# Feed-forward by seven products: products that add onto a bank, and a new order of the products

## What is computed

```python
def modulate(x, shift, scale):
    return x * (1 + scale) + shift

def swiglu(x, w13, w2):
    a, b = jnp.split(x @ w13, 2, axis=-1)
    return (jax.nn.silu(a) * b) @ w2

def ffn_half_step(h, g, shift, scale, gate, w13, w2):
    return h + 0.5 * gate * swiglu(modulate(rms_norm_2(h, g), shift, scale), w13, w2)
```

## Time and profile before

| what | us |
|---|---|
| median of 3 runs | 4607.99 |
| range of the runs | 4604.65 to 4612.93 |
| the profiled execution, its own time | 4617.37 |
| its span from first to last instruction | 4615.6 |
| TensorE busy in it | 4242.2 (92%) |
| weight loads busy | 3445.0 (75%) |
| VectorE busy | 2458.5 (53%) |
| ScalarE busy | 1471.4 (32%) |

### The profile page before, as it was taken

The page is one execution under the profiler, slowest core; times in us unless marked ns, Lnnn a source line. Parts: engine busy times, 40 slices in busy tenths (PEclk is TensorE's granted clock), DMA queues, the critical chain, the costliest instruction groups (busy, mean ns, idle before and its releaser), DMA issues. The chain is left out here.

```text
span 4615.6 us, 89015 instructions
## 1 busy us (share of the span) xinstructions
PE 4242.2 (92%) x39320; PEld 3445.0 (75%) x39320; DVE 2458.5 (53%) x3948; ACT 1471.4 (32%) x2591; POOL 94.3 (2%) x83
## 2 busy tenths in 40 slices
PE   7999999998869999799998998999989999988997
PEld 4666666667547777499997556999989999446886
DVE  4455554545122333276764353766676665345886
ACT  3323322332023444143332232333343332223443
POOL 0000000000000000000000020000000000020000
PEclk9999999999889999899999999999999999998998
DMA  3000000002343443212121101122112121202221
GB/s 143 22 22 22 22 22 21 3 22 80 132 160 147 165 157 137 109 65 73 65 74 44 67 19 55 65 74 74 55 55 77 61 73 39 100 19 80 94 101 64
DMA packets 42479, 332.02 MB, mean 72 GB/s; under 512 B 4082, under 2 KB 8563, under 8 KB 12787
## 3 DMA queue, kind: packets, MB, share of 16 engines
q1 hardware_dynamic: 42098, 326.37, 19.5%
HBM read 324.26 MB, written 2.10 MB: 71 GB/s over the span
## 5 line engine op out<-in xcount | busy, mean ns | idle before, releaser
L762 PE MATMUL banks<-x_hi,w_hi 128*128 128x384 f32 (+1 forms) x2496 | 812.5, 326 | 50.8 <-ACT ffn_tiles L879 33.6
L763 PE MATMUL banks<-x_lo,w_hi 128*128 128x384 f32 (+1 forms) x2496 | 806.9, 323 | 0.0
L764 PE MATMUL banks<-x_hi,w_lo 128*128 128x384 f32 (+1 forms) x2496 | 806.7, 323 | 0.0
L849 ACT CAST w_hi<-landing 128x512 fp32r<-128x512 f32 x768 | 466.5, 618 | 625.2 <-PE banks L764 615.9
L928 DVE TENSOR_TENSOR w_lo<-landing,w_hi 128x512 fp32r<-128x512 f32 x768 | 519.4, 685 | 72.5 <-ACT w_hi L849 69.3
L762 PEld LDWEIGHTS banks<-x_hi,w_hi 128*128 128x128 f32 x2496 | 475.5, 191 | 65.1 <-ACT ffn_tiles L879 46.3
L763 PEld LDWEIGHTS banks<-x_lo,w_hi 128*128 128x128 f32 x2496 | 475.5, 191 | 0.2
L764 PEld LDWEIGHTS banks<-x_hi,w_lo 128*128 128x128 f32 x2496 | 475.3, 190 | 0.0
L762 PE MATMUL banks<-g_hi,w_hi 128*128 128x384 f32 (+1 forms) x1232 | 421.2, 342 | 0.0
L763 PE MATMUL banks<-g_lo,w_hi 128*128 128x384 f32 (+1 forms) x1232 | 421.2, 342 | 0.0
L764 PE MATMUL banks<-g_hi,w_lo 128*128 128x384 f32 (+1 forms) x1232 | 421.2, 342 | 0.0
(11 more groups left out here) (419 smaller groups left out, 6067.2 us busy)
## 6 DMA issues: line engine op xcount, KB each, us to landing
landing<-in_w SPq DMA_DIRECT2D x132, 1024.0 KB, 4.9
arena_first<-in_ada_w SPq DMA_DIRECT2D x44, 2048.0 KB, 7.9
weight_ring_first<-in_rw_pair SPq DMA_DIRECT2D x8, 2048.0 KB, 8.8
weight_ring_first<-in_da_head SPq DMA_DIRECT2D x8, 2048.0 KB, 12.4
weight_ring_mix<-in_w_in SPq DMA_DIRECT2D x12, 1024.0 KB, 5.0
weight_ring_first<-in_ada_w SPq DMA_DIRECT2D x4, 2048.0 KB, 8.7
weight_ring_mix<-in_w_out SPq DMA_DIRECT2D x8, 1024.0 KB, 4.9
x_res<-in_x_t SPq DMA_DIRECT2D x2, 2048.0 KB, 12.2
```

The costliest lines, as they stand in the source:

```text
L762: mm(o, wh, xh, start=first, stop=False, skip_group_check=onto)
L763: mm(o, wh, xl, start=False, stop=False, skip_group_check=onto)
L764: return mm(o, wl, xh, start=False, stop=last, skip_group_check=onto)
L849: nc.scalar.copy(SH[:, q % RING], raw(q)).then_inc(whi.h, 1)
```

## The change

It changes which bank a product is made in, which engine sums, and the order of the products. Nothing is left out and no product is added.

- Three banks a group. P1 is made in bank 0 and ScalarE copies it to X1; P6 adds onto it and ScalarE copies the sum to X2; P7 adds onto it and ScalarE copies that to X3; P4, whose weights now have the opposite sign (t4 is b21 - t2), adds onto it and ScalarE takes the silu from the bank. P2 has bank 1. P5 has bank 2 and P3 adds onto it.
- VectorE adds three times in place of six: bank 1 onto X1 after P2, bank 2 onto X3 after P7 and onto X2 after P3. The two gatings follow P3.
- The order is P1, then P4 and P3 of the group before, then P2, P6, P5, P7. With a "w" unit in between, P4 and P3 follow its first slot. Slots keep their old places in the ring; `order` lists them as they are used.
- The ring is refilled by `splits_at`: after place n come those slots, in slot order, whose predecessor in the ring has been used by then. VectorE does the same one place later.

```diff
@@ -660,8 +661,9 @@
         PLAIN, RING, GR = 2, 11, 6
         A11, A21, A12, A22, S1, S2, S4 = range(7)
         S3 = A21
+        P1, P3, P2, P5, P6, P7, P4 = range(7)
         operand_of = (A11, S4, A12, S1, S2, S3, A22)
-        bank_of = (0, 1, 0, 2, 3, 4, 5)
+        bank_of = (0, 2, 1, 2, 0, 0, 0)
 
...
-        used_up = lambda q: last_slot[slots[q][3]] + 1 if slots[q][0] == "g" and slots[q][1] < PLAIN else q + 1
+        order, held = [], []
+        for kind, u in units:
+            q = begin[kind, u]
+            if kind == "g" and u < PLAIN:
+                order += [q, q + 1, q + 2, q + 3]
+            elif kind == "g":
+                order += [q + P1] + held + [q + P2, q + P6, q + P5, q + P7]
+                held = [q + P4, q + P3]
+            else:
+                order += [q] + held + list(range(q + 1, q + (8 if u < 5 else 4)))
+                held = []
+        assert sorted(order) == list(range(Q))
+        place_of = {q: n for n, q in enumerate(order)}
+        used_up = lambda q: place_of[last_slot[slots[q][3]] if slots[q][0] == "g" and slots[q][1] < PLAIN else q] + 1
+        ended = lambda kind, u, part: place_of[begin[kind, u] + part] + 1
+        splits_at, nxt = [], RING
+        for n in range(Q):
+            splits_at.append([])
+            while nxt < Q and used_up(nxt - RING) <= n + 1:
+                splits_at[-1].append(nxt)
+                nxt += 1
+            assert n + 1 == Q or order[n + 1] < nxt
...
         first_bank, at_bank = {}, 0
         for kind, u in units:
+            if kind == "w":
+                at_bank += at_bank % 2
             first_bank[kind, u] = at_bank
-            at_bank += 16 if kind == "w" else 4 if u < PLAIN else 6
+            at_bank += 16 if kind == "w" else 4 if u < PLAIN else 3
         bank_no = lambda kind, u, n: (first_bank[kind, u] + n) % 8
...
-                def group(u):
-
-                    q, s = begin["g", u], u - PLAIN
-                    for part in range(7):
-                        b, x = bank_no("g", u, bank_of[part]), operand_of[part]
-                        if part != 2:
-                            take_bank(b, *((sil_ready, 2 * u + 1), (u_made, 6 * s + 3), None, (u_made, 6 * s + 5), (u_made, 6 * s + 1),
-                                           (u_made, 6 * s + 4), (u_made, 6 * s + 6))[part])
-                        else:
-                            pe.wait_ge(p1_copied.h, p1_copied.at(0, s + 1))
-                        if s == 0 and part == 1:
-                            pe.wait_ge(sums_lo.h, sums_lo.at(0, 4))
-                        if s == 0 and part == 5:
-                            pe.wait_ge(sums_lo.h, sums_lo.at(0, 5))
-                        pe.wait_ge(wlo.h, wlo.at(0, q + part + 1))
-                        r = (q + part) % RING
-                        for k in range(4):
-                            ins = triple(bank(b), SH[:, r, k], SL[:, r, k], AH[:, x, k], AL[:, x, k], k == 0 and part != 2, k == 3, part == 2)
-                        ins.then_inc(slot_done.h, 1)
-
-                def second(c):
-
-                    q, ks = begin["w", c], tiles_of(c)
-                    pe.wait_ge(glo.h, glo.at(0, ks[-1] + 1))
-                    for n in range(KT):
-                        slot, at = (q + n, 0) if len(ks) == 4 else (q + n // 2, 2 * (n % 2))
-                        if at == 0:
-                            pe.wait_ge(wlo.h, wlo.at(0, slot + 1))
+                def quarter(q):
+
+                    _, u, part, _ = slots[q]
+                    s, b, x = u - PLAIN, bank_no("g", u, bank_of[part]), operand_of[part]
...
-                for kind, u in units:
+                for q in order:
+                    kind, u, part, _ = slots[q]
                     if kind == "w":
-                        second(u)
-                    elif u < PLAIN:
+                        second(q)
+                    elif u >= PLAIN:
+                        quarter(q)
+                    elif part == 0:
                         plain_group(u)
-                    else:
-                        group(u)
...
-                def after(q):
-                    kind, u, part, _ = slots[q]
+                def copy_product(u, x):
+                    nc.scalar.copy(x, bank(bank_no("g", u, 0))).then_inc(copied.h, 1)
+
+                def after(n):
+                    kind, u, part, _ = slots[order[n]]
+                    done = lambda: act.wait_ge(slot_done.h, slot_done.at(0, n + 1))
+                    strassen = kind == "g" and u >= PLAIN
+                    s = 3 * (u - PLAIN)
                     if kind == "g" and u < PLAIN and part < 2:
-                        act.wait_ge(slot_done.h, slot_done.at(0, q + 1))
+                        done()
                         gate_half(u, part, bank(bank_no("g", u, part)))
-                    elif kind == "g" and u >= PLAIN and part == 0:
-                        act.wait_ge(slot_done.h, slot_done.at(0, q + 1))
+                    elif strassen and part == P1:
+                        done()
+                        if u == PLAIN:
+                            act.wait_ge(sums_lo.h, sums_lo.at(0, 4))
+                        else:
+                            act.wait_ge(sil_ready.h, sil_ready.at(0, 2 * u - 1))
+                        copy_product(u, X1)
+                    elif strassen and part == P6:
+                        done()
                         act.wait_ge(g_ready.h, g_ready.at(0, 2 * u - 1))
-                        nc.scalar.copy(X1, bank(bank_no("g", u, 0))).then_inc(p1_copied.h, 1)
-                    elif kind == "g" and u >= PLAIN and part == 2:
-                        act.wait_ge(slot_done.h, slot_done.at(0, q + 1))
-                        gate_half(u, 0, bank(bank_no("g", u, 0)))
-                    elif kind == "g" and u >= PLAIN and part == 6:
-                        act.wait_ge(u_made.h, u_made.at(0, 6 * (u - PLAIN) + 6))
-                        gate_half(u, 1, X2)
-                    if q and slots[q - 1][0] == "g" and slots[q - 1][1:3] == (slots[q - 1][1], 3 if slots[q - 1][1] < PLAIN else 6):
-                        g_high(slots[q - 1][1])
-                    if q == begin["g", PLAIN] - 1:
+                        copy_product(u, X2)
+                        act.wait_ge(u_made.h, u_made.at(0, s + 1))
+                        gate_half(u, 0, X1)
+                    elif strassen and part == P7:
+                        done()
+                        act.wait_ge(g_ready.h, g_ready.at(0, 2 * u))
+                        copy_product(u, X3)
+                    elif strassen and part == P4:
+                        done()
+                        gate_half(u, 1, bank(bank_no("g", u, 0)))
+                    if n and slots[order[n - 1]][0] == "g" and slots[order[n - 1]][2] == (3 if slots[order[n - 1]][1] < PLAIN else P3):
+                        g_high(slots[order[n - 1]][1])
+                    if n == begin["g", PLAIN] - 1:
                         x_sums(4)
-                    if q + RING < Q:
-                        split(q + RING)
+                    for q in splits_at[n]:
+                        split(q)
...
                         if part == 2:
-                            tt(t4, t2, b21, ALU.subtract).then_inc(wsum.h, 1)
-
-                def combine(u, op, out, b, other):
-                    s = 6 * (u - PLAIN)
-                    tt(out, bank(bank_no("g", u, b)), other, op).then_inc(u_made.h, 1)
+                            tt(t4, b21, t2, ALU.subtract).then_inc(wsum.h, 1)
+
+                def add_bank(u, x, b):
+                    tt(x, bank(bank_no("g", u, b)), x, ALU.add).then_inc(u_made.h, 1)
...
-                def after(q):
-                    kind, u, part, _ = slots[q]
-                    s = 6 * (u - PLAIN)
-                    done = lambda: dve.wait_ge(slot_done.h, slot_done.at(0, q + 1))
-                    made = lambda n: dve.wait_ge(u_made.h, u_made.at(0, s + n))
+                def after(n):
+                    kind, u, part, _ = slots[order[n]]
+                    s = 3 * (u - PLAIN)
+                    done = lambda: dve.wait_ge(slot_done.h, slot_done.at(0, n + 1))
                     if kind == "w":
...
-                    elif u >= PLAIN and part == 4:
+                    elif u >= PLAIN and part == P2:
                         done()
-                        dve.wait_ge(p1_copied.h, p1_copied.at(0, u - PLAIN + 1))
-                        combine(u, ALU.add, X2, 3, X1)
-                        made(1)
-                        combine(u, ALU.add, X1, 2, X2)
-                        made(2)
-                        combine(u, ALU.add, X1, 1, X1)
-                    elif u >= PLAIN and part == 5:
+                        dve.wait_ge(copied.h, copied.at(0, s + 1))
+                        add_bank(u, X1, 1)
+                    elif u >= PLAIN and part == P7:
                         done()
-                        combine(u, ALU.add, X2, 4, X2)
-                        made(4)
```

(18 more changed lines are left out.)

61 lines of the change are left out of this document (45 added, 16 removed).

## The result

The changed kernel takes 4883.8 us (median of 6 runs, 4876.0 to 4892.2) against 4611.0 us of the kernel before on the same chip (6 runs, 4604.7 to 4616.4): a ratio of 1.0593, with a 95% interval from 1.0583 to 1.0604. It is 273 us slower. The forecast was 4885.

A forecast was written before the change was run, and what follows sets the result against it. TensorE's pace was taken to bound the blocks. New waits of 226 us plus 87 of slow clock less 36 for the old wait gave +277 us, forecast 4885 us against the median of 4608.0, range 4750 to 4965.

The forecast's parts named there:

- ScalarE takes its list in turn: On ScalarE, a ready copy doesn't pass instructions that wait ahead of it; the old copy stood behind a silu waiting 4.27 us.
- The walk through a row of seven: After P3, seven splits delay the copy of P6; TensorE loses 3.0 us before P7, 3.85 in the last block.
- Ahead of "w": Before a "w" unit the row's last split waits for a load: copy 4.55 us late, 5.5 us in the last block.
- the price of a copy: ScalarE's copies take 0.47 us by the row; the page's 0.62 us for 384 would add 9 us in all.
- The number: How many waits before P7: 30 and 15 ahead of "w" in the first three blocks, 10 and 5 in the last.
- The sum of the waits: TensorE's new waits before P7 cost 226 us, 192 to 260; the old wait's going gives 36 back.
- the first waits of the blocks: The first group's P6 in each block waits for the copy as P2 did: 10.3 us in all, which stay.
- The clock: TensorE's clock falls in the new waits: 1.0 us each at 2.7 us, 1.9 for the others, 87 us in all.
- The clock did not hold: Rival: the splits stall TensorE but its clock stays up, 4798 us; chance 0.20.
- The copies after one product did not pinch: Rival: rows of seven are hidden, but TensorE waits for two copies after one product each, 4645 us; chance 0.06.
- the change's own gain, 4572: Rival: ScalarE's copy of P6 is ready in time, so 36 us go and nothing comes, 4572 us; chance 0.06.
- the old wait: In the kernel before, P2 waits for ScalarE's copy of P1, 46.4 us in all; 36 us go with the change.

The follow-up runs named there:

- e1: Changed kernel with the last two splits of sum-waiting rows put behind the copy of P6, and the load-waiting split behind the copy of P7: 4606.3 us, ratio 0.9988.
- e3: Changed kernel with only the split that waits for a load ahead of "w" units put behind the copy of P7: 4760.4 us, ratio 1.0319.
- e8: Kernel before, with its splits gathered into rows of seven after P4 in 15 groups of each block: 4742.2 us, ratio 1.029.
- e4: Changed kernel with matmuls nobody reads put ahead of P7's wait in 15 groups of each block: 4814.4 us, ratio 1.0441.
- e5: Changed kernel with rows of seven dealt out after P3, P2 and P7, and four early splits put behind the copy of P1: 4579.4 us, ratio 0.9928.
- e6: Kernel before, with ScalarE's copy of P1 put ahead of the second silu of the group before: 4578.0 us, ratio 0.9928.
- e7: Changed kernel with each row of seven splits left whole but put behind the copy of P6: 4679.7 us, ratio 1.0154.

## Why the prediction was right, step by step

**ScalarE takes its list in turn.** Right, and all else rests on it. At 2137.25 a copy ended whose input P6 had been there since about 2132.5; e1 moves what stood ahead, and the wait is gone.

**The walk through a row of seven.** With zero at 2128.19 it had put t1's split at 5.4, t2's at 7.36, `g_high` at 7.88, the copy at 8.62 and its end at 9.09. The rows read 5.40, 7.33, 7.86, 8.59 and 9.06. TensorE was forecast 2.9 us late; the row's idle time of 2.71 us is counted from the modelled end of a matmul, 0.16 us after the next could have started, so it was 2.87. Ahead of "w" 4.55 had been forecast, and the 15 waits read 4.2 to 4.6 idle, 4.4 to 4.7 late. In the last block 3.75 and 5.4 stood against an idle time of 3.54 in ten and 5.1 to 5.3 in five, 3.7 and 5.2 to 5.5 late.

On the price of a copy the prediction names the page ScalarE: Activation LUTs of the Trainium skill, section Rules for kernel authors. The budget there is for an ACTIVATE whose bias is a pointer operand, and not for a plain copy. Its 0.62 us is no price for these copies; those of 128x384 took 0.47.

**The number.** 30, 15, 10 and 5, as forecast.

**The sum of the waits.** By the starts of the matmuls (without the waits for x at the start of a block) the waits cost 42 us before and 234 after: +192, where the sum had 226 - 36 = 190. Within it two terms were off by about 4 and 6 us against each other: the 60 waits come to some 222 us rather than 226, and the first waits of the blocks didn't stay as they were. They grew from 9.1 to 14.8 us idle (3.32, 3.42, 3.00 and 5.07), which the prediction had put at no change with the words "they stay". The copy of P1 at 2007.14 stands behind a split that had waited 1.64 us for t1; before the change the copy of P1 at this place stood behind no such wait.

**The clock.** Over the same starts the slow pace cost 16 us before and 99 after, +83, where 87 stood. The reason given for 1.0 us a wait at 2.7 us was that it lay near a row that had cost nothing. That was a guess between 0 and 2.5, and that it came out is in part luck. Of the 30 such waits 13 were followed by the slow pace (six of ten in the first block, three and four in the next two), which lost 26 us in all, or 0.87 a wait. In e3 the same 30 waits were followed by it 20 times and lost 38 us, 1.27 a wait. And the row at 2.64 us, from which the guess was taken, was one draw: in e8 half of the waits of 1.84 us cost the clock. One wait in the first block that left the clock as it was and one that took it down, each in 8 us from near P7's start (the idle time is in neither but for 1.3 us of the second):

```profile
2034.00:2042.00 8.00, 8.00 (x48) 8.00 (x47) 1.77 (x4) 2.65 (x6) 0.00 (x0) 1.00 0.00 0
2136.00:2144.00 8.00, 6.70 (x22) 6.70 (x23) 3.41 (x6) 2.15 (x5) 0.00 (x0) 0.57 0.03 12
```

All those of 3.0 us and more went with the slow pace. So the figure of 1.0 was near the mean and wrong as a description of any one wait. For the 30 longer waits ahead of a P7 the slow pace came to 56 us, where 57 stood. That the clock's share is real, and not a reading of the pace, e4 shows with its 69 us.

**The rivals.** The clock did not hold (4798 would have been the time). The copies after one product did not pinch: TensorE has no wait ahead of a P6 beyond the first of a block, nor ahead of a P4. And the change's own gain, 4572, is what e5 reaches (4579) once the rows are dealt out, so the 36 us put down for the old wait were about right. But e6 has the same from the old kernel, which the prediction hadn't looked at: the old wait was one of order alone.

**What I missed beyond the forecast** was VectorE's side of the repair in e1, and the growth of the first waits. Both are the same kind of error: an edit's place was read on one engine's list, and the work on which it depends stands in the other's.

## What to carry to other kernels

When a ring of buffers is refilled in ring order and the order of use is changed, look at which slot is now used last: all behind it are refilled in one burst, on every engine that takes part, and what stands behind the burst in an engine's list waits for its slowest member. The cure here was to deal the burst out (e5), not to undo the new order. Before taking work off an engine, ask whether the bound engine waits for that work or only for its place in a list; here half of VectorE's adds of products were worth nothing that could be measured, and one copy moved past one silu was worth 33 us. And on an engine whose clock falls when it idles, a wait costs more than its length: here 83 us on top of 192.

## What the runs showed of the hardware

TensorE's clock goes down in one wait and not in another of the same length. "Down" is the lower of its two levels, 1.2 in place of 2.4 GHz: after the wait at 2137.30 matmuls of 384 columns start 0.32 us apart and not 0.17, and the granted clock over 2136 to 2144 us reads 0.57. The runs have these counts:

| idle time of TensorE, us | where | followed by the slow pace |
|---|---|---|
| 1.6 | kernel before, last block | 0 of 10 |
| 1.6 to 2.0 | e7, last block | 0 of 15 |
| 1.84 | e8, first three blocks | 15 of 30 |
| 2.71 | kernel after, first three blocks | 13 of 30 |
| 2.71 | e3, first three blocks | 20 of 30 |
| 3.54 | kernel after, last block | 10 of 10 |
| 4.2 to 5.3 | kernel after | 20 of 20 |

What decides between the waits of 1.8 to 2.7 us, these runs don't show. Filling a wait with matmuls that nobody reads keeps the clock up (e4, 0.99 over the block), and was worth 69 us there.
